# Three norms fold their squares into the stage before them; the root's guess comes straight from PSUM; three stages walk their first tiles row by row

## What is computed

```python
def rms_norm(x, w):
    xf = x.astype(jnp.float32)
    y = xf * lax.rsqrt(jnp.mean(xf * xf, axis=-1, keepdims=True) + NORM_EPS)
    return (y * w.astype(jnp.float32)).astype(x.dtype)
# first block
n = rms_norm(h, norm_mix_w);  h = h + token_mixer(n, ...)        # ends with w_out
n = rms_norm(h, norm_ffn_w);  h = h + conv_gated_mlp(n, ...)     # w_ffn_in, w_ffn_out
x = rms_norm(h, norm_final_w)
# second block
u_lat, u_ctx = modulate(rms_norm(x, g1), ...), modulate(rms_norm(ctx, g1), ...)
x = x + g1 * (mix(u_lat, u_ctx) @ w_out)
x = x + g2 * (square(relu(modulate(rms_norm(x, norm2_g)) @ w_mlp1)) @ w_mlp2)
return rms_norm(x, final_norm_g)
```

## Time and profile before

| what | value |
|---|---|
| median of 3 runs | 3469.44 us (3467.95 to 3469.53) |
| the profiled execution's own time | 3457.17 us |
| its span, first to last instruction | 3455.0 us |
| TensorE clock granted, mean | 0.974 of full speed |
| PE busy | 3254.4 us (94%) |
| DVE, ACT, POOL busy | 55%, 47%, 56% |

### The profile page before, as it was taken

The page is one execution under the profiler, slowest core; times in us unless marked ns, Lnnn a source line. Parts: engine busy times, 40 slices in busy tenths (PEclk is TensorE's granted clock), DMA queues, the critical chain, the costliest instruction groups (busy, mean ns, idle before and its releaser), DMA issues.

```text
span 3455.0 us, 60127 instructions
## 1 busy us (share of the span) xinstructions
PE 3254.4 (94%) x21444; PEld 2931.7 (85%) x21444; DVE 1888.0 (55%) x3084; ACT 1621.0 (47%) x2348; POOL 1951.1 (56%) x2680
## 2 busy tenths in 40 slices
PE   5999999999899999999997998999989999999998
PEld 3999999999887888888875987999978788888886
DVE  4666655666466754763775664555555443434343
ACT  4555544555335444443434555655543444434343
POOL 3767776677454555554541445888855455555553
PEclk7999999999999999999998998999989999999999
DMA  4666666666385555555643755767648455555553
GB/s 161 228 219 206 217 201 212 209 204 221 132 295 167 188 178 187 183 178 187 186 152 132 255 194 200 238 208 228 210 138 316 153 188 188 184 184 186 185 188 104
DMA packets 262408, 673.13 MB, mean 195 GB/s; under 512 B 28263, under 2 KB 66888, under 8 KB 261448
## 3 DMA queue, kind: packets, MB, share of 16 engines
q1 hardware_dynamic: 262152, 669.81, 58.8%
HBM read 663.38 MB, written 6.32 MB: 194 GB/s over the span
## 4 chain that ended last, share of the span: by engine, by line
PE 74%; DVE 8%; POOL 7%; issue 4%; DMA 3%; ACT 2%; SPq 1%; DVEq 0%; ACTq 0%; POOLq 0%
PE psum L645 28%; PE psum L646 14%; POOL w_lo L500 7%; PE psum L638 6%; PE psum L640 6%; PE psum L639 6%; PE psum L643 2%; PE psum L715 2%; PE psum L1446 1%; DMA ada_raw<-w_ada 1%; DVE work L769 1%; PE psum L1454 1%; PE psum L642 1%; DMA work<-w_ada 1%; DVE work L1323 1%
## 5 line engine op out<-in xcount | busy, mean ns | idle before, releaser
L500 POOL TENSOR_TENSOR w_lo<-raw,w_hi 128x256 fp32r<-128x256 f32 x2676 | 1950.9, 761 | 1474.4 <-ACT w_hi L487 1473.2
L487 ACT ACTIVATE w_hi<-raw 128x1024 fp32r<-128x1024 f32 (+3 forms) x1112 | 1051.2, 949 | 1341.9 <-PE psum L640 539.7
L638 PE MATMUL psum<-act_a,w_lo 128*128 128x256 f32 x3072 | 911.5, 297 | 31.7 <-POOL w_lo L500 14.7
L640 PE MATMUL psum<-act_a,w_hi 128*128 128x256 f32 x3072 | 875.8, 285 | 0.0
L639 PE MATMUL psum<-act_a,w_hi 128*128 128x256 f32 x3072 | 875.5, 285 | 0.0
L645 PE MATMUL psum<-act_a,w_hi 128*128 128x512 f32 x2295 | 829.5, 403 | 26.7 <-DVE act_a L757 10.6
L645 PE MATMUL psum<-act_b,w_hi 128*128 128x512 f32 x2096 | 754.0, 401 | 18.6 <-DVE act_b L1688 9.7
L500 DVE TENSOR_TENSOR w_lo<-raw,w_hi 128x1024 fp32r<-128x1024 f32 (+2 forms) x332 | 416.2, 1254 | 599.8 <-ACT w_hi L487 599.7
L646 PE MATMUL psum<-act_a,w_lo 128*128 128x256 f32 x2295 | 648.3, 282 | 0.0
L638 PEld LDWEIGHTS psum<-act_a,w_lo 128*128 128x128 f32 x3072 | 595.3, 194 | 44.9 <-POOL w_lo L500 19.2
L639 PEld LDWEIGHTS psum<-act_a,w_hi 128*128 128x128 f32 x3072 | 595.8, 194 | 3.1 <-issue 1.9
(11 more groups left out here) (343 smaller groups left out, 2916.9 us busy)
## 6 DMA issues: line engine op xcount, KB each, us to landing
raw<-w_mlp SPq DMA_DIRECT2D x256, 512.0 KB, 4.1
raw<-w_up SPq DMA_DIRECT2D x176, 512.0 KB, 3.7
raw<-w_dil SPq DMA_DIRECT2D x192, 384.0 KB, 3.3
work<-w_ada SPq DMA_DIRECT2D x288, 256.0 KB, 3.9
raw<-w_hg SPq DMA_DIRECT2D x128, 320.0 KB, 3.1
raw<-w_delta SPq DMA_DIRECT2D x64, 512.0 KB, 4.2
raw<-w_out SPq DMA_DIRECT2D x64, 512.0 KB, 5.8
raw<-w_down SPq DMA_DIRECT2D x64, 512.0 KB, 3.7
```

What stands on the lines that cost most here:

```text
L487: act.activation(w_hi[:, t % SPLIT, 0:nb * P], raw[:, t % RAW, 0:nb * P], ACT.Copy)\
L500: ins = eng.tensor_tensor(w_lo[:, t % SPLIT, cols], raw[:, t % RAW, cols], w_hi[:, t % SPLIT, cols], ALU.subtract)
L638: pe.matmul(bank[:, 0:S], wl, src[:, kt, 0:S], start=first, stop=False)
L640: return pe.matmul(bank[:, 0:S], wh, src[:, kt, S:2 * S], start=False, stop=last)
```

## The change

- `rows_first`, `turned`, `blocks0`, `evac0`: in ctx, the first up and the first mlp1, pass 0 walks its 3 or 4 tiles row by row (all tiles' block of row 0, then of row 1, and so on), and the weights lie in memory in that order. All its tiles finish in the last item, and all but the last are evacuated there (the last in the next pass's first item, as before).
- `Norm(early=True)` for norm 1 (behind out), 5 (behind out2) and 6 (behind the last mlp2): in the stage, ACT squares the tile before (128x256) at each tile, and DVE folds squares 0 to 13 into one tile (`part` in PSUM, the last fold into `total` in SBUF). Behind the meet PE multiplies only `total` and squares 14 and 15 by the ones.
- The other norms (0, 2, 3, 4) sum both halves into the same 256 columns: 16 matmuls of 256 columns for 8 of 512.
- All seven: a one-column `Abs_reciprocal_sqrt` (`warm`) runs first on ACT, so that a table load, if one is due, comes there; the root's guess reads PSUM with 1/D and eps as scale and bias; DVE refines with three `scalar_tensor_tensor`.

```diff
+def rows_first(blocks, tiles):
+    kt = KT
+    head = [blocks[k * kt + r] for r in range(kt) for k in range(tiles)]
+    return head + blocks[tiles * kt:]
...
-    out["w_ctx"] = stream(ctx, 6)
+    out["w_ctx"] = stream(rows_first(ctx, 3), 6)
...
+        self.turned = name == "ctx" or (name in ("up", "mlp1") and not done)
+        rows = [(k, kt, kt == 0, kt == KT - 1) for kt in range(KT) for k in range(self.tpb)]
+        self.blocks0 = [rows[q * nb:(q + 1) * nb] for q, (_, nb) in enumerate(items)]
+        self.evac0 = [[] for _ in items]
+        self.evac0[-1] = [(0, k) for k in range(self.tpb - 1)]
...
+            def act_square(self, act, j):
+                if j >= 2:
+                    wait(act, "norm_added", self.a0 + j - 1)
+                act.activation(self.ring[j % 2], self.src[:, j, :], ACT.Square)\
+                   .then_inc(sem("norm_square"), 1)
...
+                    m = i * ph.tpb + k
+                    if m:
+                        wait(act, "tile_out", ph.t0 + m)
+                        self.act_square(act, m - 1)
...
+            def dve_tile(self, dve, m):
+                j = m - 2
+                if j < 0:
+                    return
+                wait(dve, "norm_square", self.s0 + j + 1)
+                wait(dve, "norm_added", self.a0 + j)
+                if j == 0:
+                    ins = dve.tensor_copy(self.part, self.ring[0])
+                else:
+                    ins = dve.tensor_tensor(self.total if j == KT - 3 else self.part, self.part,
+                                            self.ring[j % 2], ALU.add)
...
             def pe(self, pe):
+                v = mix[:, 1, 0:S]
+                if self.early:
+                    wait(pe, "norm_added", self.a0 + KT - 2)
+                    pe.matmul(v, ones, self.total, start=True, stop=False)
+                    for j in (KT - 2, KT - 1):
+                        wait(pe, "norm_square", self.s0 + j + 1)
+                        ins = pe.matmul(v, ones, self.ring[j % 2], start=False, stop=(j == KT - 1))
...
-                wait(act, "norm_summed", 8 * n + 8)
-                act.activation(self.h, mix[:, 0, S:2 * S], ACT.Copy).then_inc(sem("norm_half"), 1)
-                wait(act, "norm_mean", n + 1)
-                act.activation(self.y, self.v, ACT.Abs_reciprocal_sqrt).then_inc(sem("norm_guess"), 1)
+                wait(act, "norm_summed", self.c0 + (1 if self.early else 8))
+                act.activation(self.y, mix[:, 1, 0:S], ACT.Abs_reciprocal_sqrt, scale=1.0 / D, bias=EPS)\
+                   .then_inc(sem("norm_guess"), 1)
...
-            phase(PHD["out"], None, pair_mixers("act", act, PHD["out"]))
+            phase(PHD["out"], norms[1].act_tiles(act, PHD["out"]), pair_mixers("act", act, PHD["out"]))
+            norms[1].act_last(act, PHD["out"])
```

More of the change, by code:

```diff
@@ L582, in body @@
                         split(eng, ph.next, 0, t + AHEAD - ph.ipb)
-                    for off, k in ph.evac[t] if tiles else ():
+                    for off, k in (ph.evac0 if first and ph.turned else ph.evac)[t] if tiles else ():
                         if not (first and off < 0):
@@ L626, in block @@
             def block(i, t, b):
-                k, kt, first, last = ph.blocks[t][b]
+                turned = ph.turned and isinstance(i, int) and i == 0
+                k, kt, first, last = (ph.blocks0 if turned else ph.blocks)[t][b]
                 if hidden and k == 0 and isinstance(i, int) and i == 0:
@@ L695, in build, with __init__ @@
         class Norm:
-            count = splits = 0
-            def __init__(self, src, gain, dst, shift=None, plain=None):
+            count = splits = squares = sums = adds = 0
+            def __init__(self, src, gain, dst, shift=None, plain=None, early=False):
                 ar = Area(WORK - 4096)
-                self.sq, self.u = ar.take(2, 512), ar.take(4, S)
-                self.v, self.y, self.t, self.h = [ar.take(S) for _ in range(4)]
+                self.sq, self.u, self.y, self.warm = ar.take(2, 512), ar.take(4, S), ar.take(S), ar.take(1)
+                self.ring = [self.sq[:, 0, 0:S], self.sq[:, 0, S:2 * S]]
+                self.total, self.part = self.sq[:, 1, 0:S], mix[:, 2, 0:S]
@@ L704, in __init__ @@
                 self.src, self.gain, self.dst, self.shift, self.plain = src, gain, dst, shift, plain
-                self.n = Norm.count
+                self.early = early
+                self.n, self.m = Norm.count, Norm.splits
+                self.s0, self.c0, self.a0 = Norm.squares, Norm.sums, Norm.adds
                 Norm.count += 1
-                self.m = Norm.splits
                 Norm.splits += plain is None
-                self.chain = "norm_dve_steps"
-            def pe(self, pe):
-                n = self.n
+                Norm.squares += KT if early else 8
@@ L718, in act @@
             def act(self, act):
                 n = self.n
-                for j in range(8):
+                act.activation(self.warm, ones[:, 0:1], ACT.Abs_reciprocal_sqrt)
+                for j in range(0 if self.early else 8):
                     if j >= 2:
-                        wait(act, "norm_summed", 8 * n + j - 1)
+                        wait(act, "norm_summed", self.c0 + j - 1)
                     act.activation(self.sq[:, j % 2, :], self.src[:, 2 * j:2 * j + 2, :], ACT.Square)\
@@ L2573, in _ @@
             dve.wait_ge(sem("x_loaded"), 80)
[L2574 removed]
+            phase(PHD["out"], dve_residual(dve, PHD["out"], norm=norms[1]), pair_mixers("dve", dve, PHD["out"]))
             meet(dve, "dve", "out_done")
```

62 lines of the change are left out of this document (38 added, 24 removed).

## The result

| | median (range), us | against before in the same comparison |
|---|---|---|
| the changed kernel, 6 runs | 3442.86 (3434.53 to 3444.39) | 0.9926 [0.991, 0.9942] |
| before, 6 runs beside it | 3468.69 (3460.09 to 3471.67) | |
| the same changed kernel once more, beside 11 runs of before (3461.91) | 3438.37 | 0.9935 [0.9921, 0.9949] |

The change makes the kernel faster by 25.7 us (20 to 31) in the first comparison and by 22.5 us (18 to 27) in the second. The profiled execution of the changed kernel took 3441.66 us with a span of 3439.8 us.

A forecast was written before the change was run, and what follows sets the result against it. PE is busy 94%, so time can be won only where it stands still, around the norms, or runs at half clock. Terms -21.2 - 2.1 + 2.1 + 0.3 + 4.6 = -16.3 gave 3453.1 us, range 3444 to 3460.

The forecast's parts named there:

- early sums: Norms 1, 5 and 6: last residual to first scaled row falls to 4.6 us, gaining 7.4, 6.9 and 6.9, together 21.2.
- the slower rival (the rings bind): Stages with early squares: fold and square come onto PE's path at each of 48 tiles, +26 us, 3495; chance 0.05.
- turned passes: First passes of up, mlp1 and ctx: no gain, costs of 2.1 and 0.3 us at the ends, 4.6 by the clock.
- the pass's end: End of pass 0: all tiles finish together, costing 1.07 us each in up and mlp1, 0.3 in ctx.
- The half clock behind the gate: Up and mlp1, after PE's wait for item 3: PE's clock falls to half, costing 2.3 us each, 4.6 together.
- they cannot start item 3 sooner: Up and mlp1: item 3's split stands behind all 16 rounded rows, so PE reaches it after 15.2 us; gain 0.
- The size of the gap: PE's wait before item 3 of up and mlp1 grows from 1.53 to about 4.0 us.
- part 2: The new guess in norms 0, 2, 3 and 4: 0.3 + 0.4 + 1.1 + 0.3 = 2.1 us gain.
- the rival theory: Set up for the experiments, no chance given: the gain beyond the forecast comes from the turned passes or from the guess.
- The small terms: Sums in 32 short instead of 16 long instructions: 7.1 against 7.50 us in norm 2, the other three win 0.2 to 0.3.
- The clock at norm 2: Norm 2: PE waits 1.5 us longer before its sum; if the clock falls, the sum goes from 7.5 to about 10.
- Sum to row: Norms, behind the sum up to the first scaled row: 2.0 us instead of 3.55, or 3.13 without the table load.

The follow-up runs named there:

- held: The changed kernel with item 3 of ctx, the first up and the first mlp1 split at the end of the stage before: 3420.63 us, ratio to before 0.9875.
- nowarm: The changed kernel without the one-column warming activation: 3439.84 us, ratio to before 0.9943.
- held_noturn: The same as held, but without the turned passes: 3424.48 us, ratio to before 0.989.
- turnonly: The kernel before with the turned passes alone added: 3470.8 us, ratio to before 1.0017.

## Why the prediction was right or wrong

**The direction and the early sums: right.** The chain from the last residual to the first row was forecast at 4.6 us and is 4.63 in norm 1; in norms 5 and 6 it is 4.4. The three places give 6.3 to 7.6 us in three executions where 6.9 and 7.4 were forecast. The terms inside differ a little: PE's products take 1.58 to 1.79 for 1.40, and there is less between the square and PE (0.08 in norm 1 for 0.28). The squares and folds in the stages cost nothing that the traces show, so the slower rival (the rings bind) is out.

**The turned passes: right in sign and total, wrong in ctx.** Forecast 7.0 us loss; the runs have 5.9 alone and 8 in the changed kernel. By the traces up and mlp1 lose 7 to 9 us together and ctx some 3 at its first pass, of which 1 to 2 are left at its end. The forecast gave ctx 0.3: it costed only the copy at the pass's end, not the gap at item 3 that grew from 4.54 to 7.75 and more. Of the steps: the pass's end 1.07 forecast, 0.93 and 1.02 measured. The half clock behind the gate 2.3 forecast; 4.10 us at 0.58 and 4.40 us at 0.57 make (1 - 0.58) x 4.10 = 1.7 and (1 - 0.57) x 4.40 = 1.9. The step that "they cannot start item 3 sooner" holds, but item 3 came 0.9 us later, 16.08 for 15.15, which was costed at 0: POOL took 4.75 us over item 3's four pieces where it took 3.80. The size of the gap was low, "about 4.0 us" for 4.75 and 6.75: in mlp1 PE has done its 24 blocks (48 instructions at a clock of 0.84, the stretch from 2687.60 above) by 2697.88, 10.3 us after the first, where 11.2 was forecast, and item 3 came at 17.00 us, 16.05 before. The late item (0.9 us twice) costs more than the shorter half clock saves (1.0 in all). The Trainium skill (TensorE: Matmul & The Clock Gate, HAM oscillation) advises, for kernels that wait between K-tiles, to do all K-tiles of one tile before the wait. Behind gaps of 4.75 and more the trace agrees; in held, where that wait is gone, the same walk has a clock of 0.89 over its first 15.3 us and pays in up and mlp1.

**The guess: the step that failed.** It is the term of part 2 that says of norms 0, 2 and 4 that the load "now stands ahead of the first square, uncovered: 1.28 + 0.2 more there against 1.5 less behind, so 0". The 1.5 less behind is there (1.62 measured); the 1.48 more ahead is 0.10 or less (norm 2: 1.87 against 1.77; norm 4: 1.41 against 1.32). Three such terms are 4.1 us. The other half of the rival theory, that the guess is worth more, is what the runs bear out. I had taken the load for an instruction that waits with the engine's program, behind the meet; in all traced places but norm 1 of nowarm it runs as soon as ACT reaches it, and ACT reaches it while its next activation is still waiting for somebody else. Rows that would have told it were in the trace of before, in the stages behind norm 0:

```profile
46.32 1.28 ACT L1145 ACT_TABLE_LOAD   x1
53.57 0.41 ACT L1145 ACTIVATE work<-work 32x256 f32<-32x256 f32 x1 [5.96 <-DVE work L1086]
```

There too the load is long done when its activation stops waiting. With 0.10 in the three terms the sum is -16.3 - 4.1 = -20.4, inside both intervals, and the time 3449.0. That is the one step that the runs show wrong in the direction of the miss; it is 4.1 of the 9.4 us by which the first comparison went beyond the forecast.

**The small terms.** The 32 short products were given 0.4 and 0.3 us; they save nothing. The clock at norm 2, kept for the range, did fall in two of the three executions of the changed kernel: the sum took 9.08 us where before has 7.49, though PE stood still only 0.1 us longer ahead of it. Sum to row was forecast at 2.0 and is 1.93, seven times.

**What remains.** By the runs the change is worth 22.5 or 25.7 us. The mended forecast has 20.4, and the traces' places give about as much if of the first stretch only norm 0's 1.6 us is counted: -21.6 (norms 1, 5, 6) + 7.0 (up, mlp1) - 3.1 (norms 2 to 4) - 1.6 = -19.3 in the first pair, -21.0 + 8.8 - 4.8 - 1.6 = -18.6 in the second. The rest, 2 to 6 us, is within the intervals, and its cause stays open. It may lie in the start-to-out stretch: the three traces with the old norms have 1038.0 to 1041.2 us there, the eleven with the new guess 1027.8 to 1039.6, and norm 0 accounts for 1.6. But executions of one kernel differ by as much (1028.3 to 1039.6 in the changed kernel). The reference is little of the first miss: 3469.44 against 3468.69, 0.8 of the 10.2 us between 3453.1 and 3442.86. In the second comparison, where before has 3461.91, it is 7.5 of 14.7. Executions of one kernel differ by up to 18 us (before: 3457.50 to 3475.27 in one comparison). The traces put at least part of that down to the granted clock: from 28 us to the end of out it is 0.96 on average in the changed kernel's first execution (1039.6 us) and 0.98 in its third (1028.3), and 0.01 of 1000 us is 10 us. What lowers it was not tried.

## What to carry to other kernels

Cost an instruction where its own operands and semaphores let it run, not where it stands: a table load with no wait of its own was free, in all but one place here, ahead of an instruction that waits, and cost its full time behind one. An order of loops that "has less to wait for" gains nothing while the item it waits for is behind a fixed queue, and pays with PE's clock; move the item first (here into a free slot: 18 to 21 us by the runs with the turned passes; 4 to 5 without, which is inside the interval), then reorder, and judge each stage by itself: ctx lost by it either way. And judge a change by differences within one comparison: the reference itself lay at 3461.9 to 3469.4 in five sets of runs.

## What the hardware did that I had not expected

- The load of a table ran 2 us ahead of the activation that it was for, and across the meet in time (1848.17, PE's last tile ended at 1849.21). At norm 1 of nowarm it did not run ahead but began only when PE's sum had ended (1031.37), though ACT had been free for 1.81 us. What makes the difference is open.
- POOL's four pieces of item 3 took 4.75 us in the changed kernel, 3.80 in before and 4.01 in held. They follow how long DVE was at its own 128x1024 splits meanwhile. Over the first passes of up and mlp1 in all 14 traces it is 3.0 us beside 0.8 us of them (held_noturn), 3.8 beside 1.8 to 1.9, 4.0 beside 2.1 (held) and 4.74 beside 2.9 (every turned pass with the gate). No run changes this overlap alone.
- Clock at norm 2: the sum of 32 short products took 9.08 us in one execution of the changed kernel and 7.52 in another, behind the same wait of 1.87 us. The granted clock was 0.81 and 1.00. Of the 14 traces five have the short time, behind waits of 1.77 to 3.20 us, and nine 9.05 to 9.15, behind 1.77 to 3.20 as well (turnonly, with the 16 long products, has 9.13). So here the wait's length does not decide whether 1.6 us are lost.
